# A two-layer diffusion backbone on one core: filter tiles ahead of weights in the prologue, and table products, x group by group and a four-group output in the boundaries

## What is computed

```
def sandwich_update(x, y_mix, mod, g, w1, w2):
    x = x + mod[2] * rmsnorm(y_mix, g[1])
    h = modulate(rmsnorm(x, g[2]), mod[3], mod[4])
    return x + mod[5] * rmsnorm(sq_relu_mlp(h, w1, w2), g[3])
...
    h = jnp.sin(freq[0] * (feats @ w1 + b1))          # hyena_filters
    h = jnp.sin(freq[1] * (h @ w2 + b2))
    h = (h @ w3).astype(jnp.float32).reshape(n, 2 * HY_ORDER, D_MODEL)
    return h * jnp.exp(-t * deltas[None, :])[:, None, :]
...
    for i in range(DEPTH):
        mod_l = jnp.split((sc @ ada_w[i] + ada_b[i])[:, None, :], 6, axis=-1)
        h_l = modulate(rmsnorm(x_lat, norm_g[i, 0]), mod_l[0], mod_l[1])
        # y_l = mixer(h_l): attention (i = 0) or Hyena (i = 1)
        x_lat = sandwich_update(x_lat, y_l, mod_l, norm_g[i], mlp_w1[i], mlp_w2[i])
```

## Time and profile before

| | |
|---|---|
| median of 3 runs | 1463.84 us (1463.76 to 1466.75) |
| profiled execution, its own time | 1466.13 us |
| its span in the profile | 1464.4 us |
| TensorE busy | 1368.5 us (93%) |
| VectorE busy | 894.8 us (61%) |
| ScalarE busy | 618.0 us (42%) |
| GpSimd busy | 120.8 us (8%) |
| granted TensorE clock, mean over the span | 0.971 of full |

### The profile page before, as it was taken

How to read it: one execution, slowest core, us unless ns; L and a number is a source line. 1 busy time by engine, 2 the same in 40 slices (tenths; PEclk the granted TensorE clock), 3 DMA queues, 4 the chain that set the end, 5 groups by cost and what they waited for, 6 DMA issues and landing times. The chain is left out here.

```text
span 1464.4 us, 18029 instructions
## 1 busy us (share of the span) xinstructions
PE 1368.5 (93%) x6614; PEld 1127.9 (77%) x6614; DVE 894.8 (61%) x1291; ACT 618.0 (42%) x918; POOL 120.8 (8%) x149
## 2 busy tenths in 40 slices
PE   7889998999899999999988998899989999999996
PEld 2467787988688888888868887787768888888884
DVE  7668768987665554555456899988355333333333
ACT  4545445664362332514435334333445234252441
POOL 1661120002000000000110000000100000000011
PEclk9999999999899999999989999999989999999998
DMA  9434341118256565565322122221312323232221
GB/s 366 166 139 173 94 147 49 44 33 312 93 173 205 178 203 191 185 205 176 98 75 61 70 86 87 87 80 37 118 41 87 101 94 106 88 100 100 86 86 58
DMA packets 49417, 178.48 MB, mean 122 GB/s; under 512 B 5991, under 2 KB 8359, under 8 KB 46920
## 3 DMA queue, kind: packets, MB, share of 16 engines
q1 hardware_dynamic: 46344, 164.51, 33.4%
q0 software_dynamic: 3008, 13.11, 2.8%
HBM read 164.49 MB, written 10.49 MB: 119 GB/s over the span
## 5 line engine op out<-in xcount | busy, mean ns | idle before, releaser
L1706 PE MATMUL bank<-hhi,whi 128*128 128x512 f32 (+1 forms) x936 | 351.8, 376 | 10.3 <-ACT scratch L962 5.6
L1708 PE MATMUL bank<-hhi,wlo 128*128 128x512 f32 (+1 forms) x936 | 349.2, 373 | 0.0
L1707 PE MATMUL bank<-hlo,whi 128*128 128x512 f32 (+1 forms) x936 | 349.0, 373 | 0.0
L1098 DVE TENSOR_TENSOR wlo<-raw,whi 128x1024 fp32r<-128x1024 f32 x180 | 222.9, 1239 | 94.6 <-ACT whi L682 93.4
L682 ACT ACTIVATE whi<-raw 128x1024 fp32r<-128x1024 f32 x180 | 189.6, 1054 | 214.4 <-PE bank L1708 199.4
L1706 PE MATMUL bank<-ghi,whi 128*128 128x512 f32 x576 | 225.0, 391 | 4.7 <-DVE glo L1631 2.8
L1707 PE MATMUL bank<-glo,whi 128*128 128x512 f32 x576 | 224.8, 390 | 0.0
L1708 PE MATMUL bank<-ghi,wlo 128*128 128x512 f32 x576 | 224.6, 390 | 0.0
L1706 PEld LDWEIGHTS bank<-hhi,whi 128*128 128x128 f32 x936 | 176.3, 188 | 42.1 <-ACT whi L682 9.9
L1708 PEld LDWEIGHTS bank<-hhi,wlo 128*128 128x128 f32 x936 | 176.3, 188 | 31.2
L1707 PEld LDWEIGHTS bank<-hlo,whi 128*128 128x128 f32 x936 | 176.4, 188 | 30.5
(11 more groups left out here) (259 smaller groups left out, 1993.6 us busy)
## 6 DMA issues: line engine op xcount, KB each, us to landing
raw<-in_wpack SPq DMA_DIRECT2D x180, 512.0 KB, 3.4
araw<-in_apack SPq DMA_DIRECT2D x40, 512.0 KB, 3.4
amore<-in_apack SPq DMA_DIRECT2D x36, 512.0 KB, 3.4
ablk<-in_ahead SPq DMA_DIRECT2D x8, 1024.0 KB, 12.6
spectra<-scratch SPq DMA_DIRECT2D x16, 512.0 KB, 3.2
araw<-spectra POOLq DMA_DIRECT2D x8, 1024.0 KB, 5.1
fs<-in_fw SPq DMA_DIRECT2D x2, 1024.0 KB, 11.1
x<-in_xT SPq DMA_DIRECT2D x1, 2048.0 KB, 13.5
```

The lines of the kernel that those rows point to most:

```text
L1098: TT(wlo[:, s, :], raw[:, r, :], f(whi[:, s, :]), ALU.subtract).then_inc(lo_done, 1)
L1706: mm(o, lh, rh, start=first, stop=False)
L1707: mm(o, lh, rl, start=False, stop=False)
L1708: return mm(o, ll, rh, start=False, stop=last)
```

## The change

Five edits, all on one core:

1. The four squares of x get places of their own in XSQ, and squares 2 and 3 wait for the tables' subtract (`tlo_done`, whose source one of them overwrites) and no longer for GpSimd's add.
2. In the prologue weights 1 are handled after tile 1, and weights 2 and 3 after tile 7 and the tables; tiles 2 to 7 follow each other. The high copies of weights 2 and 3 go to a place in `whi`, so the first `prep` on ScalarE waits for all four subtracts. ScalarE's copies of the odd half of transform 1 come ahead of square 2.
3. Two small matmuls stand ahead of the first adaLN block (into bank B3, which is overwritten later).
4. In a boundary, VectorE scales and adds group by group, so that the first group of x is ready before the second is scaled; the column of half 0 comes behind the third add, and the last scale behind the column. TensorE gets `keep_busy`: 3 matmuls of a filter table with itself ahead of the columns, 3 behind them and, except in the last boundary, 10 behind the root's rows. Their result is not used. The rows and the inverse of half 1 come earlier within half 0's chunks.
5. In the last boundary the four groups are two chunks by all 512 tokens, and the output goes in 8 DMAs of 256 KB.

```diff
@@ -315,7 +315,7 @@
         DEC = (raw[:, :, :].rearrange("p a (b n) -> p (a b) n", b=2), ablk[:, 1, :, :])
-        XSQ = ablk[:, 3, :, :].rearrange("p (a b) n -> p a (b n)", a=2)
+        XSQ = [ablk[:, 3, 0:2, :], ablk[:, 3, 2:4, :], tap2[:, :, :], S[:, 5:7, :]]
         GEN = (AB[:, 0, :], AB[:, 1, :], B2[:, :], B3[:, :])
@@ -417,6 +417,12 @@
             return tile[rows, at:at + 3:2, :]
+
+        def weight_copy(q):
+
+            if q < 2:
+                return ghi[LOWER, 2 * q:2 * q + 2, :]
+            return whi[LOWER, q - 2, :].rearrange("p (a n) -> p a n", a=2)
@@ -568,11 +574,11 @@
                 sp.wait_ge(x_done, 3 * X_GROUPS + i + 1)
-                for j in range(4 * (i % 2), 4 * (i % 2) + 4):
-                    sp.dma_start(out[j][:, HALVES[i // 2]], x[:, j, HALVES[i // 2]]).then_inc(x_out, 16)
+                for j in range(2 * i, 2 * i + 2):
+                    sp.dma_start(out[j], x[:, j, :]).then_inc(x_out, 16)
             for n in range(2):
                 sp.wait_ge(filt_out[n], 8 * 16)
-            sp.wait_ge(x_out, 2 * KC * 16)
+            sp.wait_ge(x_out, KC * 16)
@@ -593,7 +599,7 @@
                     pool.wait_ge(xadd_done, i)
-                TTP(XSQ[:, 0, :], XSQ[:, 0, :], XSQ[:, 1, :], ALU.add).then_inc(xadd_done, 1)
+                TTP(XSQ[0], XSQ[0], XSQ[i + 1], ALU.add).then_inc(xadd_done, 1)
@@ -606,7 +612,7 @@
                     pool.wait_ge(xadd_done, 3)
-                    TTP(XSQ[:, 0, 0:NT], XSQ[:, 0, 0:NT], XSQ[:, 0, NT:2 * NT], ALU.add).then_inc(xadd_done, 1)
+                    TTP(XSQ[0][:, 0, :], XSQ[0][:, 0, :], XSQ[0][:, 1, :], ALU.add).then_inc(xadd_done, 1)
             for t in range(QKV_UNITS + 2):
@@ -695,14 +701,14 @@
                 act.wait_ge(w3_done, 2 * q + 2)
-                A(ghi[LOWER, 2 * q:2 * q + 2, :], filter_weights(q, LOWER), ACT.Copy).then_inc(w3_copy, 1)
+                A(weight_copy(q), filter_weights(q, LOWER), ACT.Copy).then_inc(w3_copy, 1)
                 A(filter_weights(q, UPPER, fw), filter_weights(q, UPPER), ACT.Copy).then_inc(w3_hi, 1)
...
                 if q == 1 and tt == 0:
-                    act.wait_ge(w3_lo, 4)
+                    act.wait_ge(w3_lo, 2)
                 if q >= 2:
@@ -733,9 +739,8 @@
                 if i >= 2:
-                    act.wait_ge(xadd_done, i - 1)
-                A(XSQ[:, min(i, 1), :], x[:, 2 * i:2 * i + 2, :].rearrange("p a n -> p (a n)"),
-                  ACT.Square).then_inc(xsq_done, 1)
+                    act.wait_ge(tlo_done, 1)
+                A(XSQ[i], x[:, 2 * i:2 * i + 2, :], ACT.Square).then_inc(xsq_done, 1)
@@ -746,30 +751,32 @@
             A(FHI, S[:, 8, :], ACT.Copy).then_inc(fh_hi, 1)
-            weight_his(1)
             ada_line(0)
...
             filter_his(1)
-            weight_his(2)
-            weight_his(3)
-            ada_line(1)
+            weight_his(1)
             filter_his(2)
             filter_his(3)
-            act.wait_ge(table_in, 16)
-            A(thi[:, :, :], S[:, 0:6, :], ACT.Copy).then_inc(thi_done, 1)
+            ada_line(1)
             filter_his(4)
...
             ada_line(2)
+            act.wait_ge(table_in, 16)
+            A(thi[:, :, :], S[:, 0:6, :], ACT.Copy).then_inc(thi_done, 1)
             filter_his(6)
...
             ada_line(3)
+            weight_his(2)
+            filter_odd(0, 0)
+            weight_his(3)
+            filter_odd(0, 1)
             act.wait_ge(x_in, 16)
...
             x_square(1)
-            filter_odds(0)
+            act.wait_ge(w3_lo, 4)
             prep(0, 0, 0)
+            filter_odds(1)
             x_square(2)
-            filter_odds(1)
             prep(1, 1, 1)
@@ -1196,7 +1203,7 @@
                 w = filter_weights(q, LOWER)
-                TT(filter_weights(q, LOWER, fw), w, f(ghi[LOWER, 2 * q:2 * q + 2, :]), ALU.subtract).then_inc(w3_lo, 1)
+                TT(filter_weights(q, LOWER, fw), w, f(weight_copy(q)), ALU.subtract).then_inc(w3_lo, 1)
@@ -1247,24 +1254,23 @@
             sine_argument(1, P)
-            weight_sums(1)
             dve.wait_ge(fh_hi, 1)
...
             filter_tile(1)
+            weight_sums(1)
             weight_los(1)
-            weight_sums(2)
-            weight_sums(3)
-            filter_tile(2)
-            filter_tile(3)
-            weight_los(2)
-            weight_los(3)
+            for n in range(2, 8):
+                filter_tile(n)
             dve.wait_ge(thi_done, 1)
...
             dve.wait_ge(tlo_done, 1)
-            for n in range(4, 8):
-                filter_tile(n)
-            filter_outs(0)
+            weight_sums(2)
+            weight_sums(3)
+            filter_out(0, 0)
+            weight_los(2)
+            filter_out(0, 1)
+            weight_los(3)
             prep(0, 0, 0)
@@ -1445,20 +1451,24 @@
+                if b == 3:
+                    for i in range(X_GROUPS):
+                        js = slice(2 * i, 2 * i + 2)
+                        rows = B3[:, :].unsqueeze(1).broadcast_to([P, 2, NT])
+                        TT(y[:, js, :], y[:, js, :], rows, ALU.mult).then_inc(scaled_done, 1)
+                        dve.wait_ge(scaled_done, X_GROUPS * b + i + 1)
+                        TT(x[:, js, :], x[:, js, :], y[:, js, :], ALU.add).then_inc(x_done, 1)
+                    return
                 y_scale(0, 0)
+                x_add(0, 0)
                 y_scale(0, 1)
-                x_add(0, 0)
                 x_add(0, 1)
                 y_scale(1, 0)
+                x_add(1, 0)
+                x_column(0)
                 y_scale(1, 1)
-                if b < 3:
-                    x_column(0)
-                x_add(1, 0)
-                if b < 3:
-                    x_inverse(0)
+                x_inverse(0)
                 x_add(1, 1)
-                if b == 3:
-                    return
                 for h in range(2):
@@ -1469,7 +1479,7 @@
                             x_column(1)
-                        if h == 0 and j == 6:
+                        if h == 0 and j == 5:
                             x_inverse(1)
@@ -1744,6 +1754,8 @@
+            for i in range(2):
+                mm(B3[0:FH, :], S[0:NFEAT, 10, 0:FH], S[0:NFEAT, 6, :], start=True, stop=True)
             pe.wait_ge(silu_done, 1)
@@ -1782,7 +1794,7 @@
                         pe.wait_ge(xadd_done, 4)
-                        mm(B2[:, :], ones, XSQ[:, 0, 0:NT], start=True, stop=True).then_inc(xss_done, 1)
+                        mm(B2[:, :], ones, XSQ[0][:, 0, :], start=True, stop=True).then_inc(xss_done, 1)
                     if m:
@@ -1924,7 +1936,15 @@
+            def keep_busy(n):
+
+                for i in range(n):
+                    mm(SC[:, 0, :], t2hi[:, 0, 0:P], t2hi[:, 1 + i % 5, :], start=True, stop=True)
+
             def boundary(b):
+                if b == 0:
+                    pe.wait_ge(thi_done, 4)
+                keep_busy(3)
                 pe.wait_ge(yacc_done, (KC - 2) * (b + 1))
@@ -1933,7 +1953,10 @@
                 square_column(S[:, 10, :], False, True).then_inc(col_done, 1)
+                keep_busy(3)
                 root_rows(b)
+                if b < 3:
+                    keep_busy(10)
@@ -1970,7 +1993,7 @@
                                 ins.then_inc(unit_done, 1)
-                        if h == 0 and k == 5:
+                        if h == 0 and k == 3:
                             x_rows(b, 1)
...
             def out_units(u0, hi, lo, ready):

```

## The result

The changed kernel takes 1455.91 us (median of four, 1454.26 to 1456.28) against 1465.3 us in the same comparison: ratio 0.9932, interval 0.9914 to 0.9951, some 10 us less by the ratio and 9.4 by the medians. The forecast of 1452 is 3.9 us low, inside its range. The profiled execution took 1454.26 us, span 1452.2, 11.9 us less than that of before; the sum had said 12.1.

What follows compares the result with a forecast made beforehand. TensorE is busy nearly throughout, so only its waits and granted clock can be won. Prologue 5.5, boundaries 6.5 and tail 0.1 make 12.1 us off the profiled 1466.13; from the median of 1463.84 that gives 1452, range 1445 to 1458.5.

Steps and rivals of the forecast that it cites:

- The lead at transform 5: Prologue: transform 5 comes 7.4 us ahead of before, or 4.9 if the clock falls before transform 4.
- the two matmuls at the start: Prologue: delay the first adaLN block by about 2 us but raise the clock earlier; gain 0.6, bounds +1.0 and -2.5.
- The sum, 6.5: Boundaries: total gain 6.5 us, taken between 5.5 less a dip and 10.3; bounds 2 and 10.3.
- s + 6.95: Boundaries: first sums of squares end 6.95 us after VectorE's first scale starts (s), at full clock; before, 10.84.
- The products' price: Boundaries: the added table products move the first scale's start by +0.8, +0.5 and 0 us in boundaries 0, 1, 2.
- the fall behind the columns: Boundaries: if the clock falls there, the first scale starts 1.35 to 2.2 us later; gains 2.5, 2.5 and 0.5.
- the dip of 1.7: Boundaries: a clock dip in the second sums, costing 1.7 us before (5.41 against 3.72), can remain.
- The chaining: Tail: last scale and add pairs wait for one another, about 0.1 us each, 0.45 in all.
- C: Whole kernel slower: products paid, clock stays at half, 8.3 us lost; 1469.7 with a prologue gain of 2.5; chance 0.03.
- D: Whole kernel, no effect: the stall returns at the weights of the first units, queued behind the spectra; 1463; chance 0.03.
- B: Prologue gives little, its lead eaten by VectorE's chain: 2.5 + 6.5 us off, 1455; chance 0.12.
- A: Clock holds in all boundaries and before transform 4: 18.4 us off, 1445.5; chance 0.14.

Runs made afterwards that it cites:

- Experiment 5: Changed kernel with the last square of x and GpSimd's last three adds moved ahead of tile 8: 1450.59 us, ratio 0.9903 to before.
- experiment 6: Changed kernel without the two small matmuls ahead of the first adaLN block: 1452.44 us, ratio 0.9922 to before.
- experiment 9: Kernel of experiment 5, with GpSimd's second add waiting until VectorE has done the modulation: 1448.41 us, ratio 0.9887 to before.
- seven and two: Seven traces with the changed boundaries 0 to 2, 55.6 to 59.4 us; two with the old boundaries (before, prologue alone), 66.0 and 63.3.
- experiment 1: Changed kernel without any of its table products (keep_busy): 1457.17 us, ratio 0.9960 to before.
- experiment 2: Changed kernel with VectorE's old order in the first three boundaries, products kept: 1456.86 us, ratio 0.9943 to before.
- experiment 12: Changed kernel without the three products ahead of the columns and the three behind, the ten kept: 1451.22 us, ratio 0.9907 to before.
- experiment 7: Changed kernel with seven more table products between the first sums and the rows of half 0: 1454.38 us, ratio 0.9933 to before.

## Why the prediction was right, and where it was off

**Prologue.** The chain came out step by step. Transform 0 was put at 50.5 and came at 51.80: VectorE waited 0.36 to 0.55 for GpSimd's low halves ahead of five of its products, so that tile 7 ended at 47.80, not 46.7. Then transform 1 at 58.9 (59.22), tile 8 behind the modulation (a second new stall: 2.09). Transform 2 was put at 68.8 and came at 70.33, since the working left out that the clock would fall behind that stall too. Transform 3 was put at 78.05 by ScalarE's copies and came at 78.22, by then behind TensorE's own work, which had no gap since 67.16: near, but partly by luck. It ran at full clock, and transform 4, put at 90.2, came at 90.44 behind a wait for GpSimd of 4.52 (4.5) with half clock behind it (0.51). The lead at transform 5, put at 4.9, came to 4.79. Experiment 5 shows that the wait before transform 4 was GpSimd's doing, not a next limit. One term has the wrong sign: the two matmuls at the start were to give 0.6 and cost about 0.8 in the trace (experiment 6). The turns of VectorE and GpSimd are measured in experiments 5 and 9: 2.26 us for 128 x 8 elements, 0.17 without an add beside them. The Trainium skill ("SBUF — State Buffer", SBUF: two separate sides) describes a port pair that one of the two engines holds for a whole instruction while the other waits; the trace agrees.

**Boundaries.** The sum, 6.5, came out as 6.6 in the first pair of traces (66.0 - 59.4) and as 6.4 on the average of seven and two (64.6 - 58.2); single pairs give 3.9 to 10.4, so the size is right, and how near a single pair comes is chance. The division is another than the working's. The first sums were to end at s + 6.95 and end at s + 7.58: the second group's two squares come 0.57 apart, while TensorE needs 1.99 for that group, so it sets the end; the working let only the last pair count. The products' price, 0.8, 0.5 and 0, was 2.0, 0.3, -0.1 in arrival to first scale against before; the fall behind the columns, for which the text had 1.35 to 2.2, came in boundary 0 only. The first unit, put at s + 13.5, starts at s + 13.33 where the second sums keep the clock and at s + 15.01 where not: the dip of 1.7 that the text left open is there in two boundaries of three in one trace, one of three in the other.

What the working had least right is what each part earns. It let the products bring the clock back ahead of the first sums, and named no gain of the order by itself. Experiments 1 and 2 show that in one trace each either part alone brings the three boundaries down to 57.2 and 59.9, against 55.6 to 59.4 with both. With the order alone the sums start earlier, and as they are themselves dense work the clock is back before they end (5.13 to 5.79 for these sums in experiment 1, 6.55 in the earlier trace rows). Of the sixteen products, six are mere price as far as the traces show (experiment 12). What the ten add beyond the order shows in the time, 0.5% between experiments 1 and 12, and not in the boundaries' traces. So they are worth it, but where they earn it stays open.

**Tail.** 0.1 was predicted, from arrival to the end 0.4 was won (11.78 to 12.2). The chaining is as priced: in VectorE's rows above, the add that waits for its scale starts 1.26 behind it, the next scale, which waits for nothing, 1.14 behind the add. Before, where a scale stood between, the add came 2.27 behind the first of two scales, 1.14 for each. For these operations the trace so decides against what the Trainium skill says ("VectorE: DVE Perf Modes", The DRAIN you can't avoid), that a semaphore costs nothing extra.

**Sum.** 12.1 against 11.9 measured on the profiled executions, but 9.4 between the medians. The nearness on the profiles is partly luck: the two steps outside the edits, +1.8 and -1.5, cancel, and the profiled execution after, 1454.26, was the fastest of its four, 1.65 under their median. The term that was off is the last: the whole sum, read from one execution of before that lies 2.3 above the median, was taken off the median. Twenty runs of before reach from 1461.94 to 1469.37, and no second trace of before tells which stretches of half clock make the difference. Rivals C and D are out: the kernel is faster, and the lead is kept to the end. B's time, 1455, is nearer than the forecast's; against its cause speak the lead of 4.79 at transform 5 and 6.68 at boundary 0, where it had 2.5. A's clock does not hold.

## What to carry to other kernels

When an engine's order is tightened, follow the helper that is idle today: here GpSimd's adds became the limit, and moving them into its own idle time earned some 7 us more (experiment 9). Matmuls that only keep the clock up are worth their place in a wait that is there anyway, and nothing ahead of the chain; first see whether an earlier start of real work brings the clock back by itself. A gain that one trace shows as a better clock is no gain before a second trace shows it.

## What was not expected of the hardware

The same kernel gets its half-clock stretches in other places from one execution to the next, with 5.30 or 3.62 us for the same 16 matmuls. Filling the wait in which the clock fell only moved the fall, in experiment 7, to the units behind it. And a vector instruction on 128 x 8 elements, 0.17 us by itself, lasted 2.26 when a GpSimd add of 2.35 had begun just ahead of it.
